# Decoder trunk on one core: where the root of the pre-norms is applied, and who carries the sums

## The reference

```python
h = rmsnorm(x, norm_pre_mix);  ...three mixer branches, gated...
x = x + rmsnorm(mixed, norm_post_mix)            # mixed = gated @ w_mix_out
h = rmsnorm(x, norm_pre_xa)
x = x + rmsnorm(cross_attention(h, mem_n, wq, wkv, wo), norm_post_xa)
h = rmsnorm(x, norm_pre_mlp)
x = x + rmsnorm(square(relu(h @ w1)) @ w2, norm_post_mlp)
```

## Time and profile before

| | |
|---|---|
| median of 3 runs | 2857.51 us (2849.43 to 2863.36) |
| profiled execution | 2863.74 us, span 2861.9 us |
| TensorE busy | 2623.4 us (92%) |
| VectorE busy | 1586.3 us (55%) |
| GpSimd busy | 1229.4 us (43%) |
| ScalarE busy | 552.1 us (19%) |
| mean granted clock of TensorE | 0.951 of full speed |

### The profile page before, as it was taken

How to read it: one execution, slowest core, us unless ns; L and a number is a source line. 1 busy time by engine, 2 the same in 40 slices (tenths; PEclk the granted TensorE clock), 3 DMA queues, 4 the chain that set the end, 5 groups by cost and what they waited for, 6 DMA issues and landing times.

```text
span 2861.9 us, 32049 instructions
## 1 busy us (share of the span) xinstructions
PE 2623.4 (92%) x11898; PEld 2160.3 (75%) x11898; DVE 1586.3 (55%) x1699; ACT 552.1 (19%) x689; POOL 1229.4 (43%) x941
## 2 busy tenths in 40 slices
PE   8988999999999999999899997777978999999995
PEld 5777777788888888888778785566757888878884
DVE  6688676666665555666666656544566122451223
ACT  3100334311111111111122212222123100121000
POOL 0322233222222112333587675420745666666663
PEclk9999999999999999999999998888989999999998
DMA  5311121111101011333654333320432322333223
GB/s 213 110 66 66 52 81 59 45 37 37 37 37 35 31 37 66 125 129 106 231 183 144 130 105 118 111 103 7 140 105 96 101 96 96 118 118 99 98 97 96
DMA packets 84593, 268.81 MB, mean 94 GB/s; under 512 B 7856, under 2 KB 9264, under 8 KB 83504
## 3 DMA queue, kind: packets, MB, share of 16 engines
q1 hardware_dynamic: 71472, 242.75, 24.7%
q10 hardware_dynamic: 13056, 25.17, 2.7%
HBM read 223.85 MB, written 44.04 MB: 94 GB/s over the span
## 4 chain that ended last, share of the span: by engine, by line
PE 73%; DVE 15%; issue 5%; ACT 4%; DMA 3%; DVEq 0%; POOL 0%; ACTq 0%; SPq 0%; POOLq 0%
PE ps L344 21%; PE ps L345 21%; PE ps L346 21%; PE xb L463 3%; DVE xx L703 1%; DVE nacc L697 1%; DMA xs<-x_d 1%; DVE lxc L893 1%; PE ps L400 1%; DVE xx L689 1%; DVE macc L697 1%; PE ps L390 1%; DVE xa L833 1%; DVE lgx L700 1%; DVE lga L915 1%
## 5 line engine op out<-in xcount | busy, mean ns | idle before, releaser
L1709 POOL TENSOR_TENSOR w_lo<-w_raw,w_hi 128x1024 fp32r<-128x1024 f32 x312 | 804.3, 2578 | 26.1
L1706 POOL TENSOR_TENSOR small<-small 128x1 f32<-128x1 f32 x312 | 87.8, 281 | 1568.6 <-PE ps L346 1378.8
L344 PE MATMUL ps<-h_hi,w_hi 128*128 128x512 f32 x1408 | 565.1, 401 | 22.0 <-DVE ub L700 20.0
L345 PE MATMUL ps<-h_lo,w_hi 128*128 128x512 f32 x1408 | 555.0, 394 | 0.0
L346 PE MATMUL ps<-h_hi,w_lo 128*128 128x512 f32 x1408 | 554.5, 394 | 0.0
L344 PE MATMUL ps<-yb_hi,w_hi 128*128 128x512 f32 x1024 | 408.4, 399 | 31.7 <-DVE yb_lo L685 22.6
L345 PE MATMUL ps<-yb_lo,w_hi 128*128 128x512 f32 x1024 | 403.4, 394 | 0.0
L346 PE MATMUL ps<-yb_hi,w_lo 128*128 128x512 f32 x1024 | 402.8, 393 | 0.0
L1707 POOL TENSOR_SCALAR w_hi<-w_raw 128x1024 fp32r<-128x1024 f32 x312 | 349.1, 1119 | 0.0
L344 PEld LDWEIGHTS ps<-h_hi,w_hi 128*128 128x128 f32 x1408 | 269.2, 191 | 82.3 <-issue 25.4
L344 PE MATMUL ps<-hx_hi,w_hi 128*128 128x512 f32 x768 | 304.9, 397 | 18.0 <-DVE hx_lo L685 17.9
(11 more groups left out here) (252 smaller groups left out, 3046.8 us busy)
## 6 DMA issues: line engine op xcount, KB each, us to landing
w_raw<-wall SPq DMA_DIRECT2D x312, 512.0 KB, 3.5
gst<-gate_d SPq DMA_DIRECT2D x24, 512.0 KB, 4.4
w_kv<-wall SPq DMA_DIRECT2D x16, 512.0 KB, 3.9
x_d<-xx ACTq DMA_DIRECT2D x16, 512.0 KB, 5.2
xs<-x_d ACTq DMA_DIRECT2D x16, 512.0 KB, 4.3
gate_d<-sigb SPq DMA_DIRECT2D x12, 512.0 KB, 2.6
gate_d<-gbuf SPq DMA_DIRECT2D x12, 512.0 KB, 2.8
x_sb<-xT SPq DMA_DIRECT2D x2, 2048.0 KB, 15.7
```

Source lines behind the costliest of these rows:

```text
L344: nc.tensor.matmul(out, wh, xh, start=start, stop=False)
L345: nc.tensor.matmul(out, wh, xl, start=False, stop=False)
L1706: nc.gpsimd.tensor_tensor(small[:, 13:14], small[:, 12:13], small[:, 12:13], ALU.add)
L1709: nc.gpsimd.tensor_tensor(w_lo[:, u], w_raw[:, u], w_hi[:, u].bitcast(F32), ALU.subtract).then_inc(w_split, 1)
```

## The change

The queries and the MLP-up products take x times gain, without the root. For the MLP the root multiplies the product in the ReLU's place; for the queries, a row of scores belongs to one token, so the root goes into the softmax's scale as a column per token (`token_roots`). The second sum of a chain is thus needed only behind the product it belongs to, and its product with ones moves to the end of the half stage; the first one's moves forward to between the two products of the first pair.

ScalarE now writes `xx` straight from PSUM, scaled by the gain, and frees the bank; VectorE only adds squares. The sums live in `xb` in PSUM until the last addition, which writes `nacc`. The residual's multiply covers two tiles at once. The old x has four buffers (`xs_of`), loaded ahead of the chain; `nt` has two. In all plain MLP-up stages VectorE does ReLU times root from PSUM and frees the bank, ScalarE squares in place.

```diff
+        xs_of = (xs_mix, xs_mix, xs_xa, xs_xa, xs_xa, xs_end)      # [P, 4, 2, HALF] each
+        sums = [xb[:, h * HALF:(h + 1) * HALF] for h in range(2)]
 # TensorE
-                half_pair(m, 0, hi, lo)
-                norm_stat(h, q)
-                half_pair(m + 1, 1, hi, lo)
-                half_pair(m + 2, 0, hi, lo)
-                norm_stat(h, q + 1)
-                half_pair(m + 3, 1, hi, lo)
+                half_pair(m, 0, hi, lo, (lambda: post_stat(c)) if c is not None else None)
+                for j in range(1, 4):
+                    half_pair(m + j, j % 2, hi, lo)
+                if c is not None and c < 4:
+                    pre_stat(c)
...
 # VectorE
+            def post_sums(c, j):
...
+                    if t < KB - 1:
+                        add(sums[h], sums[h], sqm[:, u]).then_inc(sum_used, 1)
+                    else:
+                        add(nacc[h][:], sums[h], sqm[:, u]).then_inc(nacc_ready[h], 1)
+            def residual(c, j):
...
+                    both = rn[h][:].rearrange("p (o n) -> p o n", o=1).to_broadcast([P, 2, HALF])
+                    last = s.at(mul(pair, pair, both))
...
+                s.wait(last)
+                dve.wait_ge(xs_loaded[j], 16 * (c + 1))
+                sub(pair, xs_of[c][:, j], pair).then_inc(x_new, 1)
+            def pre_low(c, j):
...
+                    dve.wait_ge(hn_hi_done, KB * c + t + 1)
+                    ins = v.scalar_tensor_tensor(lo[h][:, t], xx[h][:, t], par[:, t, gain:gain + 1], hi[h][:, t].bitcast(F32),
+                                                 ALU.mult, ALU.subtract)
+            def chain(c, pair):
+                q = 2 * (c // 2) + 1
+                root(c, q)
+                residual(c, 0)
+                residual(c, 1)
+                pair(0)
+                pre_low(c, 0)
+                residual(c, 2)
+                pre_low(c, 1)
+                pre_sums(c, 0)
+                residual(c, 3)
+                pre_low(c, 2)
+                pre_sums(c, 1)
+                pair(1)
+                pre_low(c, 3)
+                pre_sums(c, 2)
+                pre_sums(c, 3)
+                pair(2)
+                pair(3)
+                root(c, q + 1)
...
+            def up_relu(m, h, b, j, r):
+                for u in range(2):
+                    n = KB * (FFB * h + b) + 2 * j + u
+                    dve.wait_ge(mm_done, 2 * m + u + 1)
+                    if b or h or type(j) is not int or j:
+                        dve.wait_ge(ff_split, n - 1)
+                    v.scalar_tensor_tensor(sqm[:, u], half_bank(u, r), 0.0, rn[h][:], ALU.max, ALU.mult).then_inc(evac[u], 1)
+            def first_up(m0, h, j):
+                if j:
+                    up_low(h, 0, j - 1)
+                up_relu(m0 + j, h, 0, j, j % 2)
+            def last_chain(c, pair):       # c = 4, 5: no second norm; root, residual x4 with the pairs between
...
 # ScalarE
+            def post_evict(c, j):
...
+                    a.activation(sqm[:, u] if t else sums[h], half_bank(u, j % 2), ACT.Square).then_inc(sq_done, 1)
+                    a.activation(xx[h][:, t], half_bank(u, j % 2), ACT.Identity, scale=par[:, t, gain:gain + 1]).then_inc(evac[u], 1)
+            def new_x(c, j):
...
+                act.dma_start(rows_pair(x_d, j, h), pair).then_inc(x_stored, 16)
+                if c % 2 == 0:
+                    load_residual(c + 1, j)
+                for u in range(2):
+                    a.activation(hi[:, t], xx[h][:, t], ACT.Identity, scale=par[:, t, gain:gain + 1]).then_inc(hn_hi_done, 1)
+                if j > 1:
+                    act.wait_ge(xn_used, 3 * c + j - 1)
+                a.activation(nt[j % 2][:], pair, ACT.Square).then_inc(xnsq_done, 1)
+            def chain(c, pair):
+                norm_root(c, q)
+                pair(0)
+                new_x(c, 0)
+                new_x(c, 1)
+                new_x(c, 2)
+                pair(1)
+                new_x(c, 3)
+                pair(2)
+                pair(3)
+                norm_root(c, q + 1)
```

More of the change, by code:

```diff
@@ L656, in _ @@
                 for kind, b in MLP_ORDER:
[L657 to L666, removed]
+                    if kind == "up" and b == 0:
+                        half_stage(n0, yb_hi[h], yb_lo[h], 3 + h)
+                    elif kind == "up":
+                        half_tiles(n0 // 2, yb_hi[h], yb_lo[h])
                     else:
                         pe.wait_ge(ff_split, KB * (FFB * h + b + 1))
-                        with_norm(n0, hx_hi[b % 2], hx_lo[b % 2])
+                        half_tiles(n0 // 2, hx_hi[b % 2], hx_lo[b % 2])
                     n0 += KB
-            norm_stat(1, 5)
+            post_stat(5)
         @block.vector
@@ new lines, in pre_low @@
+            def pre_low(c, j):
+                h, gain = c % 2, (G_PRE_XA, G_PRE_MLP)[c // 2]
+                hi, lo = ((hx_hi, hx_lo), (yb_hi, yb_lo))[c // 2]
+                for u in range(2):
+                    t = 2 * j + u
+                    dve.wait_ge(hn_hi_done, KB * c + t + 1)
+                    ins = v.scalar_tensor_tensor(lo[h][:, t], xx[h][:, t], par[:, t, gain:gain + 1], hi[h][:, t].bitcast(F32),
+                                                 ALU.mult, ALU.subtract)
+                ins.then_inc(hx_split, 1)
@@ L1161, in new_squares, with pre_sums @@
+            def pre_sums(c, j):
+                h = c % 2
+                sq = nt[j % 2]
                 dve.wait_ge(xnsq_done, 4 * c + j + 1)
                 if j == 0:
-                    ins = add(nacc[h][:], nt[:, 0], nt[:, 1])
+                    ins = add(sums[h], sq[:, 0], sq[:, 1])
                 else:
[L1165 to L1186, removed]
@@ L1188, in renorm @@
-            def renorm(c, pairs):
-                h, gain = c % 2, (G_PRE_XA, G_PRE_MLP)[c // 2]
-                hi, lo = ((hx_hi, hx_lo), (yb_hi, yb_lo))[c // 2]
[L1192 to L1204, removed]
@@ L1206, in beside @@
-            def beside(c, q, pair):
-                h = c % 2
-                pair(0)
-                recip(h, q)
-                residual(c, (0, 1))
+                    dve.wait_ge(xn_used, 3 * c + j)
+                    done(add(sums[h], sums[h], sq[:, 0]))
+                    ins = add(sums[h] if j < 3 else nacc[h][:], sums[h], sq[:, 1])
+                ins.then_inc(xn_used if j < 3 else nacc_ready[h], 1)
+            def chain(c, pair):
[3 more added lines that the diff above has]
+                residual(c, 1)
+                pair(0)
+                pre_low(c, 0)
[5 more added lines that the diff above has]
+                pre_sums(c, 1)
@@ L1614, in queries_high @@
                     copy(yb_hi[h][:, t], half_bank(u, j % 2)).then_inc(q_hi_done, 1)
+            act.wait_ge(mm_done, N_MIX)
             for j in range(4):
-                squares(0, 0, j)
-            beside(0, 1, lambda j: squares(1, 1, j))
-            beside(1, 1, lambda j: queries_high(0, j))
+                load_residual(0, j)
+            for j in range(4):
+                post_evict(0, j)
+            chain(0, lambda j: post_evict(1, j))
+            chain(1, lambda j: queries_high(0, j))
             for j in range(4):
```

230 lines of the change are left out of this document (120 added, 110 removed).

## The result

| | before | changed |
|---|---|---|
| median, us | 2853.47 (2847.85 to 2863.36, 4 runs) | 2762.98 (2761.69 to 2764.27, 4 runs) |
| ratio | | 0.9679, 95% interval 0.9649 to 0.971 |
| profiled execution (span) | 2863.7 (2861.9) | 2764.3 (2762.5) |
| TensorE busy | 2623.4 us (92%) | 2600.5 us (94%) |
| VectorE, GpSimd, ScalarE busy | 1586, 1229, 552 us | 1525, 1218, 575 us |

90.5 us faster over the medians; 2776 was forecast, 2752 to 2803 as the range. The kernel before was profiled in the slowest of its four executions, so the two profiles differ by more, 99.4 us. A second run of the changed kernel on another occasion gave 2764.0 (ratio 0.9706, 0.9681 to 0.973).

A forecast was written before the change was run, and what follows sets the result against it. TensorE, 73% of the chain, bounds the kernel, stopped by the norms' serial chain. Savings of 21.5 + 22.5 + 17.5 + 3 + 14 + 8 = 86.5 took 2863.7 to 2777, stated as 2776 us, range 2752 to 2803.

The forecast's parts named there:

- the second stop: Norms before queries and MLP: TensorE's wait for the low half of the normalised x, 9.10 us, goes.
- the layout: One chain from a stage's start: last low at 41.8 us, last sum 44.6, stage's end 47.1.
- The new bank wait in the queries' first half: VectorE frees the second pair's bank at 39.7 us, TensorE needs it at 35.4: 4.3 wait, some 1.5 slow clock.
- The MLP's: First half's first up stage: bank wait of 10.4 us, 15.6 over in all; whole MLP -14.
- Late splits: GpSimd's weight splits late in a chain: 1.2 us, then 0.3 to 0.7 for three tiles, together 2.6.
- Loads: Early loads of the old x: little saved in chains (4.5 us of VectorE wait at most), -8 at the end.
- Sums in PSUM: Each VectorE sum takes a steady 0.69 us and stops costing up to 2.2 beside GpSimd's weight split.
- Attention: Exponential with scale from a column: up to 0.1 us x 32, between 0 and 3; 1 taken, dropped in rounding.
- its own case: The change's parts as laid out by hand: 2776 us, 2764 to 2790, chance 0.54.
- the rival without a pinch: VectorE and GpSimd interleave better than the hand layout, no bank is late: 2748 us, chance 0.21.
- the pinch: Rival: VectorE always asking for the port, a tile takes 6.6 us, 1.2 over, bank waits grow: 2803, chance 0.22.
- The slower case: MLP's bank release exceeds TensorE's 10.9 us a pair, or the stops remain: 2865 us or more, chance 0.03.

The follow-up runs named there:

- e4: Changed kernel with the second sum's product with ones asked for behind the third pair instead of the fourth; 2804.2 us.
- e3: Changed kernel with loads of the old x two ahead (one in chains 4 and 5) instead of a chain ahead; 2777.0 us.
- e5: Kernel before with only the four buffers for the old x and their early loads; 2839.5 us, ratio 0.9932.
- e2: Changed kernel with the running sums in SBUF (nacc) instead of PSUM; 2787.3 us.
- e6: Changed kernel with sums back in SBUF and late loads of the old x together; 2795.2 us.
- e7: Changed kernel with pair(1) earlier in chains 1 and 3, pair(2) earlier in chain 3, chain 3's second-sum product and root behind the second MLP-up stage; 2757.5 us.
- e8: Kernel before with only the running sums in PSUM instead of SBUF; 2846.9 us, ratio 0.997.
- e1: Changed kernel with VectorE's pair(1) behind residual(3) in chain 1 and ahead of it in chain 3, instead of behind sum(1); 2764.4 us.

## Why the prediction was right

By its own terms (us, measured from the rows of after against those of before):

| term | forecast | measured |
|---|---|---|
| mixer output, second half | -21.5 (to 47.1) | -22.4 (68.6 to 46.2) |
| queries, first half | -17.5 (to 52.5) | -17.5 (70.0 to 52.5) |
| queries, second half | -3 | -2.6 (46.5 to 43.9) |
| attention | 0 (a term of 1, dropped) | -1.4 (107.0 to 105.6) |
| attention output, second half | -22.5 (to 47.1) | -23.4 (69.6 to 46.2) |
| MLP | -14 | -17.2 (727.4 to 710.2) |
| end | -8 | -9.2 (30.3 to 21.0) |
| stages ahead of the mixer output | 0 | -5.5 |

- *What bounds it, and that the second stop goes*: right; e4 puts the stop back and gets the price that the layout gave. The slack it left (second sum at 44.6, asked for at 47.1) was 2.4 us in the trace: 1736.69 against 1739.07.
- *The new bank wait in the queries' first half*: right in place and size. The text had VectorE's pair(1) at 39.7 us and TensorE there at 35.4; VectorE's timeline of the changed kernel has it 37.6 us into the stage (start 1739.52):

```profile
1766.33 2.89 DVE L701 TENSOR_TENSOR xb<-nt 128x512 f32<-128x512 f32 x1
1769.13 1.25 DVE L704 TENSOR_TENSOR xx<-xx,rn 128x1024 f32<-128x1024 f32 x1
1770.41 1.95 DVE L707 TENSOR_TENSOR xx<-xs_mix,xx 128x1024 f32<-128x1024 f32 x1
1772.28 3.54 DVE L1186 SCALAR_TENSOR_TENSOR hx_lo<-xx,par,hx_hi 128x512 fp32r<-128x512 f32 x2
1775.75 1.42 DVE L701 TENSOR_TENSOR xb<-xb,nt 128x512 f32<-128x512 f32 x2
1777.08 1.28 DVE L689 TENSOR_TENSOR yb_lo<-ps,yb_hi 128x512 fp32r<-128x512 f32 x2
```

  TensorE got there at 35.0 and stood 3.4. What held pair(1) longest are the two lows (3.54 us together) and the first sum (2.89): undisturbed they take some 0.74 each and 0.69, and here GpSimd's split runs beside them.
- *The MLP's*: right in place, too long in size. 10.4 us were forecast; 6.90 came. ScalarE's first pair costs the chain 2.4 us and not 3.3 (the first low at 19.5 us instead of 17.1 in the queries), and part was made up behind it: GpSimd waited 2.27 us for a weight tile (its next split begins at 2055.48), and VectorE's third subtraction beside it took 1.23 us where it took 3.30 in the queries. So this term came out smaller partly by an accident that the layout did not have. The forecast had said that a weight tile may land late behind a burst of loads; one did, though only GpSimd and not TensorE waited for it.
- *Late splits*: 2.6 us a chain were forecast, 1.8 came (46.2 less 43.5 less 0.9). The tile forecast late by 1.2 was late by 1.1 (due at 1693.33 + 16.8, next product at 1711.19); of the three behind it, one (by 0.2 at 1728.05) shows. The prediction named waits for `w_lo` of some 10 us as a sign; they went from 2.1 to 4.8 us in the whole span. The granted clock is 1.00 in the mixer and attention outputs, as it said.
- *Loads*: the end right (9.1 in e3 for the steps alone). What they do in the MLP's second half was not seen. The prediction put VectorE's waits for loads at 4.5 us at most; that is the chains of the mixer output alone. In chains 2 to 4 it waited another 9.7, 5.11 of it in one go in chain 4. Early loads alone remove TensorE's wait there (e5), and so does the rest of the change without them (e3 has late loads and no wait there). In the sum it stood once, so no harm came of it.
- *Sums in PSUM*: given no number of its own in the sum; a sum was to take a steady 0.69 us. It is 20.6 us of A within the change and 6 alone. The rule of the Trainium skill that stood beside it (SBUF — State Buffer, "SBUF: two separate sides") holds in each of these runs: 680 to 700 ns with PSUM on one side, up to 2892 for the same additions in SBUF in e2.
- *Attention*: put at nothing, and that is not what happened. The exponential with its scale from a column takes 564 ns where it took 474 (0.1 was forecast), and TensorE waits 35.4 us in attention where it waited 32.0. The stretch still got shorter because the granted clock was 0.86 and not 0.80. That is luck, not the change.

So the gain of 94 us from the mixer output on is: 64 for roots, evictions and order (e6), 20 for the sums (e2), 9 for the loads at the end (e3). The forecast's 86.5 was 7 short in these, and another 5.5 us came from stages that the change doesn't touch. Both misses go the same way, which is why 2776 stood 13 above the median. The 5.5 are luck: the profile that the forecast started from is some 10 us above the median of the kernel before, for causes that are told at the end. Over the medians the gain is 90.5. 2763.0 is also 1 us below the 2764 to 2790 that the prediction gave to its own case. The mechanism is the one described, but the time lies at its edge, towards the rival without a pinch. Of the rivals, the pinch exists (the waits for banks and splits are its form), but smaller than even the forecast had it: e7 wins back 14 us of it. The slower case showed nowhere: no plain up stage of the MLP has a wait.

## What to carry to other kernels

A norm ahead of a linear product needs its root only behind the product, so the sum of squares can take the whole product to get ready: lay out when it is ready and when it is asked for, and give it two or three microseconds. A cover that hides one wait exposes the next: work out when each bank is due, and put its release ahead of work that nobody awaits. Where VectorE and GpSimd meet at the SBUF port, count turns: here running sums in PSUM won 20 us, and cutting long multiplies in two lost 9.

## What the runs showed of the hardware that was not expected

**A race at the port that is worth 7 us.** The stage ahead of the mixer output has the same instructions in all kernels, and yet it starts the mixer output between 1648 and 1661 us. One cause can be read. Near 1600 us VectorE has four instructions with two SBUF inputs in a row (two `hx_lo`, two `yst`), and GpSimd's short first instruction of a tile either waits behind the second `hx_lo` or slips in ahead of it. In the changed kernel it waits (0.74 us), and VectorE's two `yst` and its `yb_lo` take 2.13 and 1.37. VectorE's timeline, then GpSimd's, then TensorE's:

```profile
1600.35 2.13 DVE L704 TENSOR_TENSOR yst<-cdev,crs 128x512 f32<-128x512 f32 x2
1604.45 1.37 DVE L689 TENSOR_TENSOR yb_lo<-yst,yb_hi 128x1024 fp32r<-128x1024 f32 x1 [1.98 <-ACT yb_hi L1384]
```

```profile
1599.73 0.74 POOL L1764 TENSOR_TENSOR small<-small 128x1 f32<-128x1 f32 x1 [1.06 <-PE ps L351]
```

```profile
1606.16 0.49 PE L349 MATMUL ps<-yb_hi,w_hi 128*128 128x512 f32 x1 [1.07 <-DVE yb_lo L689]
```

In the kernel before it slips in (0.19 us), although it starts only 0.04 us earlier against `yst` (1598.25 to 1598.91; 1599.73 to 1600.35 above). GpSimd's long instructions then come between VectorE's, which take 4.34 and 3.25. TensorE waits 5.20 us for `yb_lo` instead of 1.07, and from there to the mixer output's start it takes 46.5 us instead of 43.7, at the slow clock behind the stop: 7.0 us in all.

```profile
1598.91 4.34 DVE L700 TENSOR_TENSOR yst<-cdev,crs 128x512 f32<-128x512 f32 x2
1605.22 3.25 DVE L685 TENSOR_TENSOR yb_lo<-yst,yb_hi 128x1024 fp32r<-128x1024 f32 x1 [1.97 <-ACT yb_hi L1344]
```

```profile
1598.25 0.19 POOL L1706 TENSOR_TENSOR small<-small 128x1 f32<-128x1 f32 x1 [1.05 <-PE ps L346]
```

```profile
1608.81 0.79 PE L344 MATMUL ps<-yb_hi,w_hi 128*128 128x512 f32 x1 [5.20 <-DVE yb_lo L685]
```

In all thirteen profiled runs a start of 1648 to 1651 goes with the first form (TensorE's wait 1.07 to 1.09) and one of 1655 to 1661 with the second (5.19 to 5.20). The form does not go with the change: e8, built on the kernel before, has the first, and e1, built on the changed one, the second. What makes the rest of the spread (1655.2 to 1661.5 within one form) was not followed.

**Attention's length is its clock.** The same 371 matmuls with nearly the same waits of TensorE (32.0 and 32.8 us) take 107.0 us at a mean granted clock of 0.80 in the kernel before and 96.1 at 0.93 in e8. Windows of the two (us, busy PE, PEld, DVE, ACT, POOL, clock, DMA, GB/s):

```profile
1882.00:1993.00 111.00, 78.97 (x371) 65.48 (x370) 54.43 (x153) 36.71 (x90) 6.44 (x5) 0.80 0.03 10
```

```profile
1872.00:1972.00 100.00, 67.12 (x371) 56.63 (x370) 54.59 (x153) 36.65 (x90) 6.74 (x5) 0.93 0.03 11
```

The pauses in it are 0.3 to 2.9 us long; after some of them the clock falls to 1.2 GHz and after some it stays at 2.4 (stretches of 8 us in the kernel before have means from 0.56 to 1.00). What decides was not tested. Together with the race it can hide an improvement of some 10 us in a median of four executions: e1's 8.7 us in A did not show at all, and of e7's 14.1 only 5.5 did. Stretches of the trace tell such things sooner.
